# The branch sums at the end of a mix block, shared between VectorE and GpSimd

## What is computed

```python
ys = jnp.stack([y_a, y_b, y_c, y_d], axis=2)
branch = jnp.einsum('bsnc,ncd->bsnd', ys, w_branch[l])
gates = jax.nn.sigmoid(gate_pre.reshape(bsz, seq, N_BRANCH, D_MODEL) + gate_b[l])
mixed = jnp.sum(gates * branch, axis=2)
x = x + mixed @ w_out[l]
```

## Time and profile before

| | us |
|---|---|
| runs of the kernel before | 1709.17, 1700.80, 1704.93 (median 1704.93) |
| profiled execution, its own time | 1706.75 |
| span of its core in the trace | 1705.0 |
| TensorE busy / VectorE busy / GpSimd busy | 1636.3 / 1089.6 / 465.6 |

### The profile page before, as it was taken

The page is one execution under the profiler, slowest core; times in us unless marked ns, Lnnn a source line. Parts: engine busy times, 40 slices in busy tenths (PEclk is TensorE's granted clock), DMA queues, the critical chain, the costliest instruction groups (busy, mean ns, idle before and its releaser), DMA issues. The chain is left out here.

```text
span 1705.0 us, 26915 instructions
## 1 busy us (share of the span) xinstructions
PE 1636.3 (96%) x10913; PEld 1471.8 (86%) x10913; DVE 1089.6 (64%) x1544; ACT 885.2 (52%) x1385; POOL 465.6 (27%) x478
## 2 busy tenths in 40 slices
PE   7989899999989999999999999999999999999999
PEld 6867799987876878998888999899988899989997
DVE  5875656545565765665467667677646766867773
ACT  6444554434445554444446736656535583656552
POOL 2510300002340130000037915043303791414430
PEclk9989999999988999999999999999999999999999
DMA  7522466655331044765465443666546444367652
GB/s 271 169 73 76 120 171 187 192 197 195 112 123 50 12 149 123 199 187 194 143 206 173 143 131 128 185 187 194 177 150 219 157 141 148 125 176 198 177 195 74
DMA packets 287067, 265.30 MB, mean 156 GB/s; under 512 B 12256, under 2 KB 247520, under 8 KB 286944
## 3 DMA queue, kind: packets, MB, share of 16 engines
q1 hardware_dynamic: 286944, 263.59, 49.6%
HBM read 262.52 MB, written 1.05 MB: 155 GB/s over the span
## 5 line engine op out<-in xcount | busy, mean ns | idle before, releaser
L144 DVE TENSOR_TENSOR w_lo<-w_raw,w_hi 128x2048 fp32r<-128x2048 f32 (+1 forms) x242 | 562.0, 2325 | 320.2 <-ACT w_hi L143 320.0
L1874 PE MATMUL bank<-h_hi,w_hi 128*128 128x256 f32 x1984 | 565.5, 285 | 5.1 <-ACT mix_proj L480 1.3
L143 ACT ACTIVATE w_hi<-w_raw 128x2048 fp32r<-128x2048 f32 (+2 forms) x244 | 462.2, 1900 | 205.5 <-PE bank L539 117.5
L1875 PE MATMUL bank<-h_lo,w_hi 128*128 128x256 f32 x1984 | 561.2, 283 | 0.0
L1876 PE MATMUL bank<-h_hi,w_lo 128*128 128x256 f32 x1984 | 561.1, 283 | 0.0
L1874 PEld LDWEIGHTS bank<-h_hi,w_hi 128*128 128x128 f32 x1984 | 380.4, 192 | 8.3 <-issue 6.2
L1875 PEld LDWEIGHTS bank<-h_lo,w_hi 128*128 128x128 f32 x1984 | 380.6, 192 | 0.0
L1876 PEld LDWEIGHTS bank<-h_hi,w_lo 128*128 128x128 f32 x1984 | 380.5, 192 | 0.0
L466 PE MATMUL bank<-w_hi,h_hi 128*128 128x512 f32 (+1 forms) x288 | 114.8, 399 | 10.8 <-DVE w_lo L144 8.8
L2927 POOL TENSOR_TENSOR cffn_hidden<-cffn_conv 128x256 f32<-128x256 f32 x44 | 74.0, 1682 | 163.3 <-ACT cffn_conv L2957 163.3
L467 PE MATMUL bank<-w_lo,h_hi 128*128 128x512 f32 (+1 forms) x288 | 112.9, 392 | 0.0
(11 more groups left out here) (443 smaller groups left out, 2885.6 us busy)
## 6 DMA issues: line engine op xcount, KB each, us to landing
w_raw<-in_w_in SPq DMA_DIRECT2D x48, 1024.0 KB, 5.1
w_raw<-in_ffn_w_in SPq DMA_DIRECT2D x88, 512.0 KB, 5.1
w_raw<-in_w_up SPq DMA_DIRECT2D x88, 512.0 KB, 5.2
w_raw<-in_ffn_w_out SPq DMA_DIRECT2D x22, 1024.0 KB, 5.0
w_raw<-in_w_down SPq DMA_DIRECT2D x22, 1024.0 KB, 4.9
w_raw<-in_nsa_w_in SPq DMA_DIRECT2D x10, 1024.0 KB, 5.2
w_raw<-in_mem_w_kv SPq DMA_DIRECT2D x8, 1024.0 KB, 5.0
w_raw<-in_w_branch SPq DMA_DIRECT2D x8, 1024.0 KB, 5.1
```

The lines of the kernel that those rows point to most:

```text
L143: return act.activation(hi, raw, ACT.Copy)
L144: return dve.tensor_tensor(self.lo[:, cut_slot, 0:k * n], raw, hi.bitcast(F32), ALU.subtract)
L1874: pe.matmul(out, h, hi[:, f, :], start=(f == 0), stop=False)
L1875: pe.matmul(out, h, lo[:, f, :], start=False, stop=False)
```

## The change

For even j the two additions are on VectorE, right behind the products of j and before the cut and the rest of j - 1. GpSimd keeps those of odd j. `mixed_p` stays one counter, raised by both engines: so VectorE waits before its first addition until GpSimd has finished j - 1, and GpSimd waits until VectorE has finished the sums of j - 1. The buffers, the other engines and the transfers are as they were.

```diff
--- before.py
+++ after.py
@@ -2530,13 +2530,13 @@
                 pool.wait_ge(ln_pow, 1)
                 pool.tensor_tensor(ln_rstd[:, :, 1:2], ln_rstd[:, :, 0:1], free(k.half_power[:, :], [[0, T], [0, 1]]),
                                    ALU.pow).then_inc(ln_pow, 1)
-                for j in range(KD):
+                for j in range(1, KD, 2):
                     pool.wait_ge(mixed_m, 2 * j + 2)
-                    p0, p1 = part[:, j % 2, 0:512], part[:, j % 2, 512:1024]
+                    pool.wait_ge(mixed_p, 2 * j)
+                    p0, p1 = part[:, 1, 0:512], part[:, 1, 512:1024]
                     pool.tensor_tensor(p0, p0, p1, ALU.add).then_inc(mixed_p, 1)
                     pool.wait_ge(mixed_p, 2 * j + 1)
-                    pool.tensor_tensor(part[:, j % 2, 0:S], part[:, j % 2, 0:S], part[:, j % 2, S:2 * S], ALU.add)\
-                        .then_inc(mixed_p, 1)
+                    pool.tensor_tensor(part[:, 1, 0:S], part[:, 1, 0:S], part[:, 1, S:2 * S], ALU.add).then_inc(mixed_p, 1)
 
             @block.scalar
             def _(act):
@@ -2774,6 +2774,14 @@
                                           k.bank[2 * (j % 2) + n2][:, :].rearrange("p (n q) -> p n q", q=S),
                                           free(gates[:, :, :], [[KD * S, 2], [1, S]], (2 * n2 * KD + j) * S), ALU.mult)\
                            .then_inc(mixed_m, 1)
+                    if j % 2 == 0:
+                        dve.wait_ge(mixed_m, 2 * j + 2)
+                        if j:
+                            dve.wait_ge(mixed_p, 2 * j)
+                        p0, p1 = part[:, 0, 0:512], part[:, 0, 512:1024]
+                        dve.tensor_tensor(p0, p0, p1, ALU.add).then_inc(mixed_p, 1)
+                        dve.wait_ge(mixed_p, 2 * j + 1)
+                        dve.tensor_tensor(part[:, 0, 0:S], part[:, 0, 0:S], part[:, 0, S:2 * S], ALU.add).then_inc(mixed_p, 1)
                     if j >= 3 and j % 2 == 1:
                         w.cut_to(dve, mix_chunks[0] + j // 2 + 2)
                     if j:
```

## The result

The changed kernel takes 1708.95 us (median of 9 runs, 1707.03 to 1710.02), the kernel before 1704.83 (9 runs); the ratio is 1.0024, with an interval of 1.0015 to 1.0033. The forecast was 1708.5, with 0.89 on a difference too small to be told by a measurement that sees 0.5%. The loss is that small, but these runs are finer than that, and it is clear of zero.

What follows compares the result with a forecast made beforehand. TensorE, busy 1636.3 of 1705.0 us, was taken as the bound, with VectorE slower at the mix blocks' ends. Two layers at 1.78 add 3.6 to 1706.75, giving 1710.3; put against the median 1704.93, 1708.5, range 1703 to 1715.

Steps and rivals of the forecast that it cites:

- Removed from GpSimd, worth 0.55 on each of two cuts: VectorE's cuts of j = 5 and 7 shorten to 2.28 us, no longer lengthened by GpSimd's even-j additions: 0.55 and 0.54.
- Added to VectorE, 1.28 for each pair: Four times a layer VectorE gains additions of 0.68 and 0.42 us plus two gaps of 0.09: 1.28.
- The new wait for GpSimd: VectorE's wait for GpSimd's sum of j - 1: hidden at j = 4 and 6 with 0.8 us spare, 0.2 at j = 2.
- The first features: At j = 0 and 2 VectorE's idle 0.73 us absorbs most; the products of j = 3 start 0.31 later.
- The path: VectorE's cut behind j = 7 ends 1.78 us later, putting TensorE 1.78 behind; its second-chunk wait grows from 0.18 to 1.5.
- The sum: Two layers at 1.78 us each make the whole program 3.6 us slower.
- GpSimd's 1.41 for 128x512: GpSimd's 128x512 addition was read as taking 1.41 us beside the products, against 3.27 and 3.33 beside a cut.
- Hidden: Slack the timeline does not show takes up VectorE's extra 1.28 us; 1705 us, no difference; chance 0.20.
- Slower by over 0.5%: In VectorE's queue all four additions lie open (10.2 us, 1715.2), or extra GpSimd meetings at j = 4 and 6 (9.2); chance 0.09.
- GpSimd might win the ports: Idle GpSimd starts ahead of VectorE's cut, which ends about 1.3 us later; 0.2 more per cut, 0.6 a layer, 1709.7.

Runs made afterwards that it cites:

- e2: Only the additions of j = 0 and 2 moved to VectorE, GpSimd keeping the rest; ratio to the kernel before 1.0003 (0.9993 to 1.0013).
- e7: Changed kernel with the third `w_out` chunk rounded ahead of the last sum's wait and cut ahead of the rest of j = 7; ratio to before 0.9997.
- e8: Changed kernel with the second cut of `w_out` ahead of the products of j = 7; ratio to the kernel before 1.0042.
- e1: Only the additions of j = 4 and 6 moved to VectorE, GpSimd keeping the rest; ratio to the kernel before 1.0013 (1.0005 to 1.0022).
- e3: Changed kernel with an extra unread 128x1024 VectorE addition behind those of j = 4 and 6; ratio to the kernel before 1.0040.
- e4: Changed kernel with an extra unread 128x1024 VectorE addition behind those of j = 0 and 2; ratio to the kernel before 1.0036.
- e9: Changed kernel, second `w_out` cut ahead of the products of j = 7, third chunk rounded and cut ahead of the last sum; ratio to before 1.0032.
- e11: Changed kernel, second `w_out` cut ahead of j = 7's products, third and fourth chunks rounded and cut ahead of the last sum; ratio to before 0.9979.
- e6: Kernel before with the third `w_out` chunk rounded ahead of the last sum's wait and cut ahead of the rest of j = 7; ratio to before 0.9965.
- e10: The same kernel as e6, run again; ratio to the kernel before 0.9977 (0.9968 to 0.9986).

## Why the prediction was right

Point by point, by its own steps.

- **Removed from GpSimd, worth 0.55 on each of two cuts.** Right: the cut of j = 5 takes 2.28 now and 2.83 again in e2.
- **Added to VectorE, 1.28 for each pair.** Slightly too much, and the term that was off most. The durations, 0.69 and 0.42, were right; an operation that waits for its own engine's result starts 0.03 to 0.04 after it here (the products end at 1478.38 + 1.29 = 1479.67, the addition starts at 1479.70), where I had taken the 0.09 between a rest and the next products, which is still there. Measured 1.19.
- **The new wait for GpSimd.** Hidden at j = 4 and 6, as argued; 0.20 at j = 2, as argued.
- **The first features.** 0.31 forecast for the products of j = 3, 0.20 measured (7.45 to 7.65 after the first products).
- **The path.** 1.78 a layer forecast, 1.49 measured. The difference is the gaps: 0.11 at j = 3 and 2 x 0.09 after it. From the products of j = 5 to those of j = 7 it is 7.91 (8.0 forecast), the last `h_hi` comes 1.48 later against the first products (1.8 forecast). TensorE's wait at the second chunk was forecast at 1.5 and is 1.47, that before j = 6 at 1.04 and is 0.92, the others at 0.87 and 0.54, and are that. e7 and e8 show that both chains behind it, cut and last sum, were late together.
- **The sum.** 3.6 us forecast, 3.0 by the traces, 4.1 (2.6 to 5.6) by the runs. The mechanism was right in every step; that 1708.5 and the measured 1708.95 are only 0.45 apart is luck, since the sum was 0.6 too high by the traces and the measured ratio lies 1.1 above them.
- **A reading.** The prediction takes GpSimd's 1.41 for 128x512 as its time beside the products. In the kernel before, the addition from 1467.96 on runs beside products only and takes 1.29; the one of 1.41 (1473.07) begins 0.16 behind the start of a rest of VectorE (1472.91). So the 0.1 is a turn given to that rest. The sum hardly hangs on it.
- **The rivals.** *Hidden* is nearly true of j = 0 and 2 (e2: 0.22 a layer) and false of j = 4 and 6 (e1); e3 and e4 show no hidden slack in the changed kernel. *Slower by over 0.5%* asked for all four pairs to lie open or for one more meeting with GpSimd; neither happened. That GpSimd might win the ports did not happen in this kernel, but did in e9 and e11. There the cut took 1.1 longer, near the 1.3 of my working, and GpSimd's second addition was locked out, too, which my working did not have. No rest follows such a cut directly in these kernels, so the 0.2 a cut is not tested.

## What to carry to other kernels

An engine that is 64% busy can have no slack at all for some 20 us, and there each microsecond moved onto it comes out in full; look for the first row from which it never waits, and for what hangs on its last one. Where a late step is shared by two or three chains (here the cut of one weight chunk, the last sum with the next rounding behind it), one of them mended alone only moves the wait. And a weight's rounding does not belong behind a data-dependent wait in the same queue if it can stand ahead: putting it and its cut there was worth 4.0 us here (e6, e10), against the 2.9 that the moved additions cost.

## What the runs showed of the hardware

**After a long wait TensorE's granted clock can be lower.** Waits up to 1.96 us (e4) left the granted clock at 1.00 here, in both layers. After 2.64 us in e3's second layer, and 2.90 in e9's, it was about half, the lower of the two levels (1.2 GHz):

```profile
1499.00:1503.00 4.00, 3.99 (x11) 3.19 (x12) 1.79 (x2) 2.00 (x2) 1.89 (x2) 0.59 0.69 200
```

```profile
1500.00:1504.00 4.00, 4.00 (x12) 3.09 (x11) 0.69 (x1) 0.72 (x2) 0.00 (x0) 0.53 0.68 193
```

The first matmul after the wait then takes 0.80 us instead of 0.50 (e9's row above). The same waits in the first layer of these two kernels had no such effect, so it does not always happen. In e3 it lengthened the stretch by 0.5 us but cost nothing in the end: TensorE did not wait for the third and fourth chunk then, and the transposes came 49.65 us after the first products, as in the first layer (49.66). In e9's second layer they came at 50.14, against 47.31 in the first: 2.8 us. e8 (2.31 and 2.32) had less clock in both layers, down to 0.73 and 0.74 over 4 us each. The times of e8 and e9 go with it, but no run tested it by itself, and what decides whether the clock falls after such a wait is open.

**Most of the spread between the profiled executions lies ahead of this change.** The first products of the first layer start at 1032.13 us in one profiled execution (e9) and at 1041.86 in another (e8), though these kernels are the same up to there. The granted clock of the first 160 us goes with it, for e6 (products at 1032.73) and e8:

```profile
0.00:160.00 160.00, 139.96 (x739) 110.72 (x740) 112.73 (x237) 84.44 (x157) 37.31 (x70) 0.99 0.45 157
```

```profile
0.00:160.00 160.00, 141.44 (x710) 110.91 (x711) 109.40 (x234) 82.07 (x153) 37.26 (x70) 0.95 0.44 151
```

The other eleven traces line up between these: 0.99 and 1032.13 (e9), 0.98 and 1035.4 to 1035.6, 0.97 and 1035.9 to 1037.5, 0.96 and 1037.4 to 1038.8. So a single span says little about an edit of 3 us; a stretch between two events near the edit repeats to 0.02 us where no clock changes.
